# A two-layer GLA / Gated-DeltaNet trunk in fp32: a triangular inverse cut into smaller pieces, a 4 MB store moved behind other stores, the last product in other banks, and tiles on 64-byte boundaries

## The reference, cut to what matters

```python
h = concat([meta_tokens(16), x(1024)])                 # D = 1024
h = h + gla_mixer(rms_norm(h, gla_norm), ...)          # layer 0
h = h + gdn_mixer(rms_norm(h, gdn_norm), ...)          # layer 1, the one the change is mostly in
out = rms_norm(h, final_norm)[:, 16:]

def gdn_mixer(h):                                      # 8 heads, dk 128, dv 256, chunk 64
    qkv, z, beta_logit, a_logit = split(h @ w_in)      # 4096 + 2048 + 8 + 8 columns
    qkv = silu(causal_depthwise_conv(qkv, conv_w))     # width 4
    g = cumsum(log_a) in each chunk
    m = strict_lower(beta * k k^T * exp(g_i - g_j))    # 64 x 64, per head and chunk
    u, w = solve(I + m, [v * beta, k * beta * exp(g)])
    per chunk: v_new = u - w S
               o = q exp(g) S + (q k^T decay) v_new
               S = S * exp(g_last) + k_dec^T v_new     # S: 128 x 256 per head, in sequence
    return (rms_norm(o, head_norm) * silu(z)) @ w_out
```

## Time and profile before

| | us |
|---|---|
| median of three runs | 1422.35 (1421.91 to 1423.25) |
| the profiled execution | 1421.89 |
| its span, first to last instruction | 1420.1 |
| PE busy in the span | 1393.1 (98%) |
| DVE, ACT, POOL busy | 764.3, 454.9, 412.1 |
| granted TensorE clock, mean | 0.997 |

### The profile page before, as it was taken

One profiled execution on the slowest core, in us unless ns is written; L12 is line 12 of the kernel. 1 busy time (PEld: TensorE's weight loads), 2 busy tenths in 40 slices (PEclk: granted clock), 3 DMA queues, 4 the chain that ended last, 5 costly groups with the idle time before them and its releaser, 6 DMA issues.

```text
span 1420.1 us, 20905 instructions
## 1 busy us (share of the span) xinstructions
PE 1393.1 (98%) x8242; PEld 1175.2 (83%) x8242; DVE 764.3 (54%) x905; ACT 454.9 (32%) x942; POOL 412.1 (29%) x361
## 2 busy tenths in 40 slices
PE   8999999999999999999999999799999999999997
PEld 6878799978888889999999999688876777777776
DVE  5224522134454347656556798999924755444442
ACT  5334621133222244343344533321134522211121
POOL 3213134342111122222222286224242622122200
PEclk9999999999999999999999999999999999999999
DMA  5521344376445135655667355534389866555530
GB/s 195 184 89 46 90 142 150 132 267 199 157 159 185 54 85 120 123 121 120 126 165 166 71 110 91 102 98 127 118 283 250 237 186 179 152 145 149 156 90 30
DMA packets 291100, 200.51 MB, mean 141 GB/s; under 512 B 165018, under 2 KB 254250, under 8 KB 290755
## 3 DMA queue, kind: packets, MB, share of 16 engines
q1 hardware_dynamic: 284418, 187.73, 47.9%
q10 hardware_dynamic: 6592, 11.54, 2.9%
HBM read 131.93 MB, written 67.29 MB: 140 GB/s over the span
## 4 chain that ended last, share of the span: by engine, by line
PE 54%; DVE 6%; issue 1%; ACT 1%; DMA 1%; POOL 0%; ACTq 0%; DVEq 0%; POOLq 0%
PE banks L2175 17%; PE banks L2959 13%; PE banks L2238 12%; DVE gdn L2491 3%; PE banks L3015 2%; PE banks L3048 2%; PE banks L3020 2%; PE banks L3029 1%; PE banks L3003 1%; PE banks L2116 1%; PE banks L2972 1%; DMA gdn_z<-gdn 1%; PE banks L1821 1%; DVE gdn L2502 1%; DVE gdn L1665 1%
## 5 line engine op out<-in xcount | busy, mean ns | idle before, releaser
L2175 PE MATMUL banks<-hn_hi,gdn 128*128 128x352 f32 x1488 | 295.8, 323 | 0.0
L2175 PEld LDWEIGHTS banks<-hn_hi,gdn 128*128 128x128 f32 x1488 | 244.5, 188 | 3.1 <-issue 2.7
L2491 DVE SCALAR_TENSOR_TENSOR gdn<-gdn,conv_taps,gdn 128x1040 f32<-128x1040 f32 x96 | 169.5, 1765 | 28.9 <-ACT gdn L2302 26.1
L2238 PE MATMUL banks<-gdn,hn_hi 128*128 128x512 f32 x512 | 164.1, 400 | 8.5 <-ACT gdn L2288 7.5
L2175 PE MATMUL banks<-hn_lo,gdn 128*128 128x352 f32 x744 | 167.8, 320 | 0.0
L2439 POOL TENSOR_TENSOR gdn<-gdn,gdn 128x1024 fp32r<-128x1024 f32 x31 | 90.3, 2913 | 247.0 <-ACT gdn L2277 247.0
L2175 PEld LDWEIGHTS banks<-hn_lo,gdn 128*128 128x128 f32 x744 | 126.9, 188 | 0.0
L2238 PEld LDWEIGHTS banks<-gdn,hn_hi 128*128 128x128 f32 x512 | 96.7, 190 | 34.4 <-issue 12.2
L920 PE MATMUL banks<-gdn,hn_hi 128*128 128x512 f32 x384 | 120.5, 395 | 0.0
L2238 PE MATMUL banks<-gdn,hn_lo 128*128 128x512 f32 x256 | 101.8, 398 | 0.0
L2959 PE MATMUL banks<-gdn,gdn 128*128 128x512 f32 x384 | 95.5, 398 | 1.4 <-DVE gdn L3174 1.2
(11 more groups left out here) (317 smaller groups left out, 2324.3 us busy)
## 6 DMA issues: line engine op xcount, KB each, us to landing
gdn<-in_gdn_w_in SPq DMA_DIRECT2D x32, 512.0 KB, 4.2
gdn_v<-gdn SPq DMA_DIRECT2D x64, 132.0 KB, 4.0
gdn<-in_x SPq DMA_DIRECT2D x16, 512.0 KB, 4.0
gdn<-in_gla_w_in SPq DMA_DIRECT2D x32, 256.0 KB, 4.2
gdn_kq<-gdn SPq DMA_DIRECT2D x16, 512.0 KB, 4.1
gdn<-in_gdn_w_in SPq DMA_DIRECT2D x32, 256.0 KB, 4.1
gdn<-gdn_kq SPq DMA_DIRECT2D x16, 512.0 KB, 3.7
gdn<-gdn_ek SPq DMA_DIRECT2D x16, 512.0 KB, 5.6
```

The lines of the kernel that those rows point to most:

```text
L2175: return pe.matmul(acc[n % 2][:, b, 0:m], w[n % 2][:, kt, :], x[:, kt, PAD + s:PAD + s + m], start=(kt == 0 and e == 0), stop=(kt == KT - ...
L2238: mm = pe.matmul(z_bank(grp * TT + t), x[:, kt, P + t * P:P + (t + 1) * P], z_half(w, p_), start=(kt == 0 and e == 0), stop=(kt == KT - 1 ...
L2491: dve.scalar_tensor_tensor(cv[:, :], xs[:, tap:tap + L], T.cw[:, tap, t:t + 1], cv[:, :], ALU.mult, ALU.add).then_inc(S("ni_conv"), 1)
```

## The change

- `SPANS` are 352, 352 and 336 columns; every span then begins on a multiple of 64 bytes.
- The arena's base, `A_DEC` and all fp32r tiles taken in rows are rounded to 16 elements (`LINE`), so that stationary and moving tiles begin on multiples of 64 bytes.
- `invert(..., fine=True)` on DVE: the steps with s <= 8 yield after each term, 2\*(n+120) each; `PORTION` is 3200.
- The meta system's product with beta goes from DVE to POOL, behind its inverse (`ni_um`).
- z uses four buffers for the last group too.
- SP: the meta tokens' stores and loads wait for the end of the inverse alone; the coefficients of chunks 0 and 1 are stored apart (`gdn_ua_first`, two DMAs of 8 partitions each), chunk 0's loaded from there; the 4 MB store is issued when the third z group's last four stores have landed; after it come the decay factors and rows 0 and 1 of `w_out`; when it has landed, z, chunk 1's coefficients and v, then further rows.
- ACT waits for the 4 MB store after the meta tokens' eviction, DVE not at all. Tiles of the scan are placed anew: the state behind the inverse's 2\*C\*C elements, the outputs and the residual on them.
- POOL scales the meta keys before chunk 0's queries.
- `out_project` of the last token tile uses banks 0 and 1 and doesn't wait for `ns_yd`.

```diff
-SPANS = [(0, 352), (352, 344), (696, 344)]
+SPANS = [(0, 352), (352, 352), (704, 336)]
+LINE = 16
-A_DEC = GH * 2 * NT
+A_DEC = -(-GH * 2 * NT // LINE) * LINE
...
@@ def invert(dve, sem, flat, stride, size, ct, tt, tmp, fine=False)
                     step += 1
-            yield 2 * s * (n + 120)
+                if fine:
+                    yield 2 * (n + 120)
+            if not fine:
+                yield 2 * s * (n + 120)
...
@@ Arena.row
-            at = row.end
-            row.end = at + -(-math.prod(shape[1:]) // 8) * 8
+            size = math.prod(shape[1:])
+            unit = LINE if dt == F32R else 8
+            at = -(-row.end // unit) * unit
+            row.end = at + -(-size // 8) * 8
...
@@ gdn_in
         def z_slot(k):
-            return k % 4 if k < G3 * TT else 1 + k % 2
+            return k % 4
...
             sp.wait_ge(S("ni_dec_in"), 16 + 16 * NH)
-            sp.wait_ge(S("ni_u"), 4)
+            sp.wait_ge(S("ni_um"), 1)
             sp.dma_start(T.gdn_uam, m_rows).then_inc(S("ni_uam_out"), 16)
-            sp.dma_start(T.gdn_ua, sc[:, 0:2 * C * C].rearrange("p (j x) -> p j x", x=2 * C)).then_inc(S("ni_ua_out"), 16)
+            sp.wait_ge(S("ni_inv"), steps(C))
+
+        def store_first(sp):
+            sp.wait_ge(S("ni_u"), 2)
+            for c in range(FIRST):
+                sp.dma_start(T.gdn_ua_first[c], sc_x[c::NCH]).then_inc(S("ni_ua_out"), 16)
+
+        def store_ua(sp):
+            sp.dma_start(T.gdn_ua, sc_x).then_inc(S("ni_ua_out"), 16)
...
-            PORTION = 3800
+            PORTION = 3200
...
@@ gdn_scan, sync
-            sp.wait_ge(S("ni_uam_out"), 16)
             load_meta()
             load_kt(0)
+            F.store_first(sp)
+            sp.wait_ge(S("ni_ua_out"), F.ua_first)
+            load_ua(0)
             load_kt(1)
-            sp.wait_ge(S("ni_ua_out"), 16)
-            load_ua(0)
+            for k in range(F.tiles - 4, F.tiles):
+                F.z_stored(sp, k)
+            F.store_ua(sp)
             load_ek(1)
             for n in range(2):
                 sp.wait_ge(S(("ni_zhi", "ni_zlo")[n]), KT * F.tiles // TT + 4)
             load_rows(0, 1)
-            for k in range(F.tiles - 4, F.tiles + 1):
-                F.z_stored(sp, k)
+            sp.wait_ge(S("ni_ua_out"), F.ua_all)
+            F.z_stored(sp, F.tiles)
             for m in range(2):
                 tokens(sp, og[m], T.gdn_z, m * C, C, R[::-1], S(f"ns_in_z{m}"))
+            load_ua(1)
+            load_v(1)
             sp.wait_ge(S("ni_zdone"), F.tiles + 2)
-            load_rows(2, 3, 4)
+            load_rows(2, 3)
...
@@ gdn_scan, tensor, out_project
-                wait(pe, S("ns_yd"), 2 * t)
+                if t < TT - 1:
+                    wait(pe, S("ns_yd"), 2 * t)
...
@@ gdn_scan, scalar and vector
-            act.wait_ge(S("ni_ua_out"), 16)
             act.wait_ge(S("ns_mv"), 1)
             act.activation(vn[RM[0], :, :], pK[RM[0], :, :], ACT.Copy).then_inc(S("ns_mvn"), 1)
+            act.wait_ge(S("ni_ua_out"), F.ua_all)
...
-            dve.wait_ge(S("ni_ua_out"), 16)
             dve.wait_ge(S("ns_mv"), 1)
...
@@ build
-            base = -(-nc.sbuf_base // 32) * 32
+            base = -(-nc.sbuf_base // (4 * LINE)) * 4 * LINE
...
-            A, E = Arena(nc, -(-nc.sbuf_base // 32) * 32), Sems(nc)
+            A, E = Arena(nc, -(-nc.sbuf_base // (4 * LINE)) * 4 * LINE), Sems(nc)
```

More of the change, by code:

```diff
@@ L2626, in systems @@
                 dve.wait_ge(S("ni_sys"), 5)
-                yield from invert(dve, S("ni_inv"), sc[:, :], 2 * C, C, ct, tt, dm)
+                yield from invert(dve, S("ni_inv"), sc[:, :], 2 * C, C, ct, tt, dm, fine=True)
             def weigh():
@@ L2728, in gdn_scan @@
         behind.end = ahead.end
-        St = behind.take([P, NH, NDV])
         oT_hi = behind.take([P, KO, P], F32R)
         oT_lo = behind.take([P, KO, P], F32R)
-        kq_at, ek_at, St_at = 0, 2 * NH * 2 * C, ahead.end
+        og = [behind.take([P, HP, NDV]) for n in range(2)]
+        h = [behind.take([P, D])]
+        hole = behind.end
+        behind.end = FRONT + 2 * C * C
+        assert behind.end == hole + D
+        kq_at, ek_at, St_at = 0, 2 * NH * 2 * C, behind.end
+        St = behind.take([P, NH, NDV])
         last_hi = A.at(St_at, [P, KO, P], F32R)
         last_lo = [A.at(n, [P, KO // 2, P], F32R) for n in (kq_at, ek_at)]
-        og = [behind.take([P, HP, NDV]) for n in range(2)]
         vn = behind.take([P, HP, NDV])
+        ua = [behind.take([P, HP, 2, C]) for n in range(2)]
         kt = [behind.take([P, HP, NDK]) for n in range(2)]
-        ua = [behind.take([P, HP, 2, C]) for n in range(2)]
-        h = [behind.take([P, D]) for n in range(2)]
+        h.append(behind.take([P, D]))
         junk = T.hn_hi_f32[:, :, D:TP]
@@ L2788, in gdn_scan, with pY @@
         p56 = bank[:, 4:6, :]
-        pY = [bank[:, 6 + n, :] for n in range(2)]
+        def pY(t, half):
+            return bank[:, (6 if t < TT - 1 else 0) + half, :]
         pS = [[b[:, p, :].rearrange("p (h v) -> p h v", v=NDV) for p in range(2)] for b in (p56, bank[:, 0:2, :])]
@@ L2854, in load_meta @@
             def load_meta():
+                tokens(sp, vm, T.gdn_v, 0, NMETA, RM, S("ns_in_m"))
+                keys(ktm, 0, NMETA, RM, S("ns_in_m"))
+                sp.wait_ge(S("ni_uam_out"), 16)
                 for p in range(2):
@@ L2869, in chunk @@
             def chunk(m):
-                if m + 1 < NCH:
-                    load_ua(m + 1)
-                    if 1 <= m < NCH - 2:
+                if m:
+                    if m + 1 < NCH:
+                        load_ua(m + 1)
+                    if m < NCH - 2:
                         load_kt(m + 1)
@@ L2889, in chunk @@
                 if m == 2:
-                    for k in range(F.tiles + TT - 2, F.tiles + TT):
+                    for k in range(F.tiles + TT - 4, F.tiles + TT):
                         F.z_stored(sp, k)
@@ L2958, in out_project @@
                             for half in halves:
-                                mm = pe.matmul(pY[half].rearrange("p (a b) -> p a b", b=P), o,
+                                mm = pe.matmul(pY(t, half).rearrange("p (a b) -> p a b", b=P), o,
                                                w_[:, 4 * half:4 * half + 4, :], start=(i == 0), stop=(i == n - 1))
```

70 lines of the change are left out of this document (36 added, 34 removed).

## The result

| | median us | executions | lowest, highest |
|---|---|---|---|
| before | 1422.68 | 8 | 1421.91, 1423.25 |
| after | 1414.99 | 8 | 1408.64, 1416.92 |

The ratio is 0.9937, with a 95% interval of 0.9921 to 0.9953: 7.7 us off the median of before, where I had forecast 21.7. Two things stand in these lines. The profiled execution of after is the shortest, 1408.64 (span 1406.8), and even it gained 13.3 us, not 21.7. And the executions, which lay within 1.3 us of each other before, now spread over 8.3 us, with a mean granted clock of 0.999 in the shortest and 0.996 in the longest. In two later sets the median was 1411.88 (5 executions) and 1411.33 (6).

A forecast was written before the change was run, and what follows sets the result against it. PE, busy 98% of the span, was taken as the bound, through its waits and matmul start distances. Savings 12.2 + 7.9 - 0.7 + 1.1 + 1.2 = 21.7 us off 1422.35 gave 1400.6 us, range 1395 to 1409.5.

The forecast's parts named there:

- Part 1: Matmuls across the kernel: tiles and spans on multiples of 64 bytes shorten start-to-start distances, saving 12.2 us.
- Part 2: z's start: smaller DVE pieces cut PE's wait from 7.5 to 1.7 us and avoid the clock's fall, saving 7.9.
- Part 3: Scan's start: the later 4 MB store costs 0.7 us; the stall in z's last group goes, saving 1.1.
- Part 4: Last token tile's product: using other banks removes PE's wait before it, saving 1.16 us.
- A displaced moving tile costs 233.3 - 229.6 = 3.7 ns: L920's two halves: a weight piece 32 bytes past a multiple of 64 costs 3.7 ns per matmul, taken as 4.
- 4 ns off one matmul in three: Projection: the third span begins 32 bytes past; aligning it saves 4.0 us over all triples.
- Rival A: Operand places: the 32 bytes do nothing, so the time is 1412.9 us; chance 0.13.
- also lie far apart: L920's two kinds of place are far apart in SBUF, so another difference could make the 3.7 ns.
- Rival B: v's end: DVE stays late, wait 5 us and clock falls, losing 5.5 of 7.9 us, 1406; chance 0.13.
- Nothing comes back on DVE's side: DVE after z's start: its remaining six pieces start 6.5 us earlier, so the inverse ends 1 us earlier.
- hidden by 2 us: Chunk 0: the 4 MB store lands at 1058, before ACT needs it for the eviction at 1060.4.
- Rival C: Scan's start: the 4 MB store becomes the new wait; chance 0.09 up to 1409, 0.02 with the kernel slower.

The follow-up runs named there:

- e11: Changed kernel with one 4 MB store of all coefficients behind z's third group, none stored apart: median 1414.97 us.
- e2: Kernel before with only the inverse's smaller pieces on DVE and PORTION 3200: median 1423.67 us, ratio 1.0006 to before.
- e4: Changed kernel with one early store of all 4 MB of coefficients in place of the two small stores: median 1418.20 us.
- e8: Changed kernel with all tiles of the arena 64 bytes further, hn staying: median 1417.37 us.
- e10: Changed kernel without edit, run again on the chip of e6 and e9's comparison: median 1411.33 us.
- e12: Changed kernel with all tiles of the arena 32 bytes further, hn staying: median 1418.31 us.
- e1: Changed kernel without edit, profiled again: median 1411.88 us, profiled execution 1412.87.
- e6: Changed kernel with only chunk 0's coefficients stored apart, one small store instead of two: median 1409.43 us.
- e9: Changed kernel with one small store and chunk 3's v loaded ahead of w_out's rows 12 and 13: median 1407.94 us.

## Why the prediction was wrong, by its steps

| step | predicted | in the profiled execution |
|---|---|---|
| Part 1, pitches | -12.2 | -4.5 |
| Part 2, z's start | -7.9 | -9.2 |
| Part 3, z's last group and the scan's start | -0.4 | +0.7 |
| Part 4, last banks | -1.2 | -1.3 |
| two waits in layer 0 (L843, L1318), which vary by as much between executions | 0 | +0.7 |
| sum | -21.7 | -13.6 |

(-4.5 is the 4.9 of the table above less 0.4 for z's ten matmuls at 1.2 GHz, which belong to Part 2. Measured 1421.89 - 1408.64 = 13.3. The steps are taken from start to start, which makes Part 4's wait of 1.16 us 1.3. No run takes Part 4 or the meta tokens' steps out alone.)

**Part 1 failed by size, and this is the step that cost most.** "A displaced moving tile costs 233.3 - 229.6 = 3.7 ns" took two halves of one line as a law for 1500 matmuls and three kinds of operand. Only L1303 gave more than I took, 2.3 us for 1.6, and it keeps the gain with both tiles displaced. Z gave 1.0 for 3.1, the last products 1.1 for 1.9, L920 lost 0.6 where it was to gain 1.2, and the projection, "4 ns off one matmul in three", gave 0.6 for 4.0: the earlier trace rows and its counterpart are 11.36 and 11.37 us. The sum, 12.2, measured 3.3 by itself and 4.5 in the whole. Rival A, at 0.13, has the nearest time, 1412.9, and its reason is half right (there is an effect of the place, but no 64). That its time is near is in part luck: it gives Part 1 nothing, where it has 4.5 us, and what lies between the profiled execution and the median takes that and more away again. I had its main argument in the text, that L920's halves "also lie far apart", and gave it too little.

**Part 2 was right in mechanism and a little small.** Conv, pieces, transpose and split followed in the order given; PE waits 0.5 where I had 1.7, and the clock's fall went with the wait. Rival B (DVE late) didn't come. But "Nothing comes back on DVE's side" was asked of the wrong engine. What comes back is PE's lead: reaching z's third group 10 us earlier while the inverse still ends where it did (its first store at 1034.1 before, 1032.6 to 1035.8 after) makes the two streams of stores meet. By itself Part 2 is worth nothing.

**Part 3 failed by sign.** I priced one user of the late store, ACT in chunk 0, rightly ("hidden by 2 us"; measured 1.4), and took the rest as free: the two small stores "fit before chunk 0's use" (they do, but some of ACT's issues are stretched to 1.0 to 2.6 us, and 1.5 to 2.9 us of waits stand at z's end), and the loads behind the large store have users "8 us and more behind" (chunk 3's v was 6.7 to 8.6 us late on DVE and up to 2.0 late for PE). The 1.1 us of the stall that was to go became 1.5 us of another. Both are waits of a size that varies from one execution to the next, some with the clock behind them. In the two executions at 1412 to 1413 that were profiled they make the 3 to 4 us above the shortest; that they also make the first median's 6 is argued, not shown. Rival C named the place and the wrong store.

**Part 4** was right: no wait stands before the last product.

## What to carry to other kernels

A wait removed upstream moves every later meeting of transfers: before adding its gain, ask which stores and loads are pinned to another engine's end (here the inverse) and lie now beside those of the stage that came nearer, and give the two edits one price, together and each alone. A difference of 2% between two groups of matmuls is no law of placement until one group has been moved; shift all tiles by a few steps before sizing it. Margins of 1 to 2 us at DMA waits don't show in one profile, since it may be the luckiest execution: read them as part of the cost.

## What the runs showed that I had not expected

- A stand of PE of 7 to 7.5 us costs very different sums by where it falls: 4.4 us at 1.2 GHz behind it before z's 512-column products, 5.5 us in chunk 0 (e11), 14.1 us before the scan's short products and fills (e2), and as much in e4. Stands of 2.2 to 2.7 us were each followed by some 3.4 us at 1.2 GHz (e8, e10, e12), and one of 2.0 us brought none (e1: 1.00 behind 1127).
- One or two DMA issues on ACT's queue take 1.0 to 2.6 us in place of 0.52 while stores of 8 partitions are in flight, with a single such store too (1.4 us in e6, 2.2 in e9); with none in flight all are 0.52 (e11).
- The distance from start to start of identical matmuls moves by 6 ns (L1303, 512 columns, 234.3 to 228.3) with nothing changed but where their tiles lie.
- A store from 8 partitions runs as 8 packets at a time and one from 128 as 16, so a second small store waits for the first (e6, e10).
